# Sums of squares gathered in fewer steps, and the latent half of an output product kept out of the last banks

## What is computed

```python
def rms_norm(x, gain):
    y = xf * lax.rsqrt(jnp.mean(xf * xf, axis=-1, keepdims=True) + EPS)
    return (y * gain).astype(x.dtype)

# first block, each layer:
x = x + g1 * mixer(modulate(rms_norm(x, norm_gain[i, 0]), sh1, sc1))
x = x + g2 * swiglu(modulate(rms_norm(x, norm_gain[i, 1]), sh2, sc2), ffn_w_in[i], ffn_w_out[i])

# second block:
h = _rmsnorm(h_res, norm_w[l])
y_mla = _mla(...) * jax.nn.silu(g_mla)      # 1024 wide
y_na = _na(...) * jax.nn.silu(g_na)         # 1024 wide
h_res = h_res + jnp.concatenate([y_mla, y_na], axis=-1) @ w_out[l]
```

## Time and profile before

| | |
|---|---|
| time, median of 3 runs | 1233.76 us (1232.35 to 1234.3) |
| time of the profiled execution | 1234.3 us |
| its span, first to last instruction | 1232.6 us |
| mean granted TensorE clock | 0.991 of full speed |
| PE busy | 1177.3 us, 96% of the span |
| DVE busy | 706.9 us, 57% |
| ACT busy | 540.3 us, 44% |
| POOL busy | 92.9 us, 8% |
| DMA | 183.02 MB, mean 148 GB/s |

### The profile page before, as it was taken

How to read it: one execution, slowest core, us unless ns; L and a number is a source line. 1 busy time by engine, 2 the same in 40 slices (tenths; PEclk the granted TensorE clock), 3 DMA queues, 4 the chain that set the end, 5 groups by cost and what they waited for, 6 DMA issues and landing times.

```text
span 1232.6 us, 18590 instructions
## 1 busy us (share of the span) xinstructions
PE 1177.3 (96%) x7064; PEld 981.3 (80%) x7064; DVE 706.9 (57%) x1189; ACT 540.3 (44%) x1000; POOL 92.9 (8%) x137
## 2 busy tenths in 40 slices
PE   7999999999999999799998889999988999999998
PEld 4666687877878888577985789999987996799766
DVE  4534666766724333768569664455566475455673
ACT  3233422222223223544448654444446566466662
POOL 0002011122100000200000010000010000020410
PEclk9999999999999999899999999999999999999999
DMA  8889456578722223133330156565444443164220
GB/s 304 320 276 329 152 171 189 171 252 277 252 85 103 94 78 101 35 103 100 106 103 1 44 167 200 171 196 176 148 137 129 130 143 103 39 205 140 103 69 35
DMA packets 121670, 183.02 MB, mean 148 GB/s; under 512 B 4497, under 2 KB 92896, under 8 KB 121600
## 3 DMA queue, kind: packets, MB, share of 16 engines
q1 hardware_dynamic: 113888, 154.64, 38.2%
q0 software_dynamic: 7712, 27.43, 6.8%
HBM read 180.68 MB, written 1.05 MB: 147 GB/s over the span
## 4 chain that ended last, share of the span: by engine, by line
PE 83%; DVE 8%; ACT 4%; issue 3%; POOL 1%; DMA 0%; DVEq 0%; SPq 0%; ACTq 0%; POOLq 0%
PE ps L489 20%; PE ps L491 20%; PE ps L490 20%; PE ps L819 2%; PE ps L820 2%; PE ps L821 2%; PE ps L860 2%; PE ps L2201 1%; PE ps L2245 1%; ACT wh L467 1%; DVE wl L474 1%; DVE nm L1132 1%; PE ps L2533 1%; PE ps L2535 1%; DVE nrm L603 1%
## 5 line engine op out<-in xcount | busy, mean ns | idle before, releaser
L489 PE MATMUL ps<-hh,wh 128*128 128x256 f32 (+2 forms) x1272 | 425.7, 335 | 17.6 <-DVE hl L619 9.5
L474 DVE TENSOR_TENSOR wl<-raw,wh 128x1024 fp32r<-128x1024 f32 (+1 forms) x246 | 295.7, 1207 | 253.1 <-ACT wh L467 249.9
L490 PE MATMUL ps<-hl,wh 128*128 128x256 f32 (+2 forms) x1272 | 416.4, 327 | 0.0
L491 PE MATMUL ps<-hh,wl 128*128 128x256 f32 (+2 forms) x1272 | 415.4, 327 | 0.0
L467 ACT ACTIVATE wh<-raw 128x1024 fp32r<-128x1024 f32 (+1 forms) x246 | 252.6, 1032 | 272.9 <-PE ps L491 261.4
L489 PEld LDWEIGHTS ps<-hh,wh 128*128 128x128 f32 x1272 | 241.7, 190 | 59.8 <-issue 27.4
L490 PEld LDWEIGHTS ps<-hl,wh 128*128 128x128 f32 x1272 | 241.2, 190 | 22.6 <-issue 1.9
L491 PEld LDWEIGHTS ps<-hh,wl 128*128 128x128 f32 x1272 | 242.2, 190 | 21.1
L489 PE MATMUL ps<-ah,wh 128*128 128x256 f32 (+2 forms) x376 | 125.9, 335 | 1.1 <-DVE big L2018 0.8
L490 PE MATMUL ps<-al,wh 128*128 128x256 f32 (+2 forms) x376 | 124.2, 330 | 0.0
L491 PE MATMUL ps<-ah,wl 128*128 128x256 f32 (+2 forms) x376 | 124.2, 330 | 0.0
(11 more groups left out here) (241 smaller groups left out, 1442.4 us busy)
## 6 DMA issues: line engine op xcount, KB each, us to landing
raw<-in_ffn_w_in SPq DMA_DIRECT2D x44, 1024.0 KB, 5.2
raw<-in_ffn_w_out SPq DMA_DIRECT2D x22, 1024.0 KB, 4.9
raw<-in_w_in SPq DMA_DIRECT2D x22, 1024.0 KB, 5.3
big<-in_w_ada SPq DMA_DIRECT2D x16, 1024.0 KB, 9.5
big<-in_w_ada POOLq DMA_DIRECT2D x24, 512.0 KB, 4.4
ex<-in_w_ada POOLq DMA_DIRECT2D x24, 512.0 KB, 5.1
raw<-in_diff_w_in SPq DMA_DIRECT2D x12, 1024.0 KB, 5.1
raw<-in_w_out SPq DMA_DIRECT2D x8, 1024.0 KB, 4.9
```

The costliest lines, as they stand in the source:

```text
L474: ins = nc.vector.tensor_tensor(place(wl), v, place(wh).bitcast(F32), ALU.subtract)
L489: nc.tensor.matmul(o, w_hi, m_hi, start=first, stop=False, **kw)
L490: nc.tensor.matmul(o, w_hi, m_lo, start=False, stop=False, **kw)
L491: return nc.tensor.matmul(o, w_lo, m_hi, start=False, stop=last, **kw)
```

## The change

Two independent things.

1. For "ffn1" and "second" POOL adds up the squares of tiles 0 to 3 only (three additions). PE multiplies the sum in `norm_sum(3)`, called after output tile m = 5, the squares of tiles 4 and 5 in the calls after m = 6 and m = 7, and those of tiles 6 and 7 after the last tile. "ffn0" and "diff" stay as they are.
2. All eight latent halves go through bank 7, in two turns of four blocks (g = 0 to 7, each 12 matmuls): halves 0 to 3 for the four blocks in steps 5 to 12, six matmuls in every step; halves 4 to 7 for block 4 in steps 17 and 18, for block 5 in step 19, for blocks 6 and 7 after the loop. DVE adds every block into x: eight additions. Slots of halves 4 to 7 are counted as used in g = 7. The final banks begin with half 8.

```diff
-        GATHERED = ["ffn0", "diff", "ffn1", "second"]
-        N_ADDED = KD - 2
+        GATHERED = {"ffn0": KD - 2, "diff": KD - 2, "ffn1": KD - 4, "second": KD - 4}
...
-            if name in GATHERED and k >= 2:
+            if k >= 2 and name in GATHERED and k - 2 < GATHERED[name]:
                 act.wait_ge(s_added, added_before(name, max(k - 2, 1)))
             elif k >= 2:
                 act.wait_ge(s_sum, b + k - 1)
...
-            for k in range(1, N_ADDED):
+            for k in range(1, GATHERED[name]):
                 pool.wait_ge(s_sq, BASE[name] + k + 1)
...
-            if name in GATHERED and k < N_ADDED:
-                if k == N_ADDED - 1:
+            if name in GATHERED and k < GATHERED[name]:
+                if k == GATHERED[name] - 1:
                     pe.wait_ge(s_added, added_before(name, k))
...
-        PART_AT, parts = {}, [(g, k) for g in range(4) for k in range(4)]
-        for i in range(4, 15):
-            n = 1 + i % 2
-            PART_AT[i], parts = parts[:n], parts[n:]
-        assert not parts
+        PART_AT = {}
+        for x in range(8):
+            PART_AT.setdefault(5 + x, []).append(divmod(x, 2))
+        PART_AT.update({17: [(4, 0)], 18: [(4, 1)], 19: [(5, 0), (5, 1)]})
+        PARTS_IN = 6
         ROUND_AT = {2: [-2], 3: [-1], 13: [0], 14: [1], 15: [2], 16: [3]}
-        def latent_part(pe, g, k):
-
-            t, c = divmod(g, 2)
-            if g and k == 0:
+        def latent_part(pe, g, half):
+
+            turn, b = divmod(g, 4)
+            t, c = divmod(b, 2)
+            if g and not half:
                 pe.wait_ge(s_part, g)
...
+            for k in range(4 * turn + 2 * half, 4 * turn + 2 * half + 2):
+                q = OUT_Q + k
+                if b == 0:
+                    pe.wait_ge(split, q + 1)
...
+                nc.tensor.matmul(ps[:, 7, :], a_h, w_h, start=(k == 4 * turn), stop=False)
+                nc.tensor.matmul(ps[:, 7, :], a_h, w_l, start=False, stop=False)
+                ins = nc.tensor.matmul(ps[:, 7, :], a_l, w_h, start=False, stop=(k == 4 * turn + 3))
+                if b == 3:
+                    ins.then_inc(used, 1)
+            if half and b < 3:
                 ins.then_inc(s_fill, 1)
...
             na_dve(dve, link, mark)
-            split_next(dve, OUT_Q + 4, 8)
-            dve.wait_ge(s_part, 4)
+            latent_added(dve, 6)
+            split_next(dve, OUT_Q + 4)
+            latent_added(dve, 7)
+            split_next(dve, OUT_Q + 5, 7)
+            dve.wait_ge(s_part, 8)
...
-                if k >= 8:
-                    pe.wait_ge(s_os, NA_G0 + k - 8 + 1)
+                pe.wait_ge(s_os, NA_G0 + k - 8 + 1)
...
-                        nc.tensor.matmul(o, a_h, w_h, start=(k == 4), stop=False, skip_group_check=True)
+                        nc.tensor.matmul(o, a_h, w_h, start=(k == 8), stop=False, skip_group_check=True)
...
-            def na_tail(i):
-
-                if i > NA_STEPS:
-                    if i == NA_STEPS + 1:
-                        pe.wait_ge(s_mx, na_max_done(NA_STEPS - 1))
-                    out_half(i - NA_STEPS + 3)
-
-            na_pe(pe, na_tail)
-            for k in range(7, 16):
+            na_pe(pe, lambda i: None)
+            for g in range(PARTS_IN, 8):
+                for half in range(2):
+                    latent_part(pe, g, half)
+            for k in range(8, 16):
                 out_half(k)
```

More of the change, by code:

```diff
@@ L536, in build @@
                 "second": [(0, 0, L2)], "lat": [(2, 0, L), (3, L, HW)]}
-        GATHERED = ["ffn0", "diff", "ffn1", "second"]
-        N_ADDED = KD - 2
+        GATHERED = {"ffn0": KD - 2, "diff": KD - 2, "ffn1": KD - 4, "second": KD - 4}
         sq_acc = big[:, 13312:13824]
         def added_before(name, k):
-            return GATHERED.index(name) * (N_ADDED - 1) + max(k, 0)
+            base = 0
+            for other, added in GATHERED.items():
+                if other == name:
+                    return base + max(k, 0)
+                base += added - 1
         def norm_square(act, name, k):
@@ L650, in norm_sum @@
                     nc.tensor.matmul(ps[:, bank, 0:b - a], T["ones"], sq_acc[:, a:b], start=True, stop=False)\
-                        .then_inc(s_sum, N_ADDED)
+                        .then_inc(s_sum, GATHERED[name])
                 return
@@ L1279, in latent_part @@
                 pe.wait_ge(s_part, g)
[L1280 to L1292, removed]
+            for k in range(4 * turn + 2 * half, 4 * turn + 2 * half + 2):
+                q = OUT_Q + k
+                if b == 0:
+                    pe.wait_ge(split, q + 1)
+                n = slice(c * 512, (c + 1) * 512)
+                at = L2 + t * P
+                w_h, w_l = wh[:, q % SPLIT_SLOTS, n], wl[:, q % SPLIT_SLOTS, n]
+                a_h, a_l = hh[:, k, at:at + P], hl[:, k, at:at + P]
+                nc.tensor.matmul(ps[:, 7, :], a_h, w_h, start=(k == 4 * turn), stop=False)
[3 more added lines that the diff above has]
+                    ins.then_inc(used, 1)
@@ L1293, in latent_part @@
+            if half and b < 3:
                 ins.then_inc(s_fill, 1)
         def latent_added(dve, g):
-            if g == 3:
-                dve.wait_ge(used, OUT_Q + 4)
-            else:
-                dve.wait_ge(s_fill, g + 1)
-            tile = x_tok[:, g // 2, g % 2 * 512:(g % 2 + 1) * 512]
+            turn, b = divmod(g, 4)
+            if b == 3:
+                dve.wait_ge(used, OUT_Q + 4 * turn + 4)
+            else:
+                dve.wait_ge(s_fill, 3 * turn + b + 1)
@@ L1302, in latent_added @@
+            if turn:
+                dve.wait_ge(s_part, g - 3)
+            tile = x_tok[:, b // 2, b % 2 * 512:(b % 2 + 1) * 512]
             nc.vector.tensor_tensor(tile, ps[:, 7, :], tile, ALU.add).then_inc(s_part, 1)
@@ L1349, in na_pe @@
                     ins.then_inc(s_pv, 1)
-                for g, k in PART_AT.get(i, ()):
-                    latent_part(pe, g, k)
+                for g, half in PART_AT.get(i, ()):
+                    latent_part(pe, g, half)
                 tail(i)
@@ L1388, in na_dve @@
             for i in range(NA_STEPS + 6):
-                for g in range(4):
-                    if (g, 3) in PART_AT.get(i - 1, ()):
+                for g in range(PARTS_IN):
+                    if (g, 1) in PART_AT.get(i - 1, ()):
                         latent_added(dve, g)
@@ L2523, in out_half @@
                 pe.wait_ge(split, q + 1)
-                if k >= 8:
-                    pe.wait_ge(s_os, NA_G0 + k - 8 + 1)
+                pe.wait_ge(s_os, NA_G0 + k - 8 + 1)
                 for t in range(2):
-                    at = (L2 + t * P) if k < 8 else t * P
-                    a_h, a_l = hh[:, k % 8, at:at + P], hl[:, k % 8, at:at + P]
+                    at = t * P
+                    a_h, a_l = hh[:, k - 8, at:at + P], hl[:, k - 8, at:at + P]
                     for c in range(2):
```

## The result

The changed kernel takes 1241.88 us in the median of its runs (1240.16 to 1246.73) against 1234.57 us for the kernel before in the same comparison (1232.35 to 1235.86); the ratio is 1.007, 95% interval 1.005 to 1.0092, that is 6 to 11 us more. The profiled execution is the fastest one seen of it, 1238.1 us with a span of 1236.4. So a reading of its total alone would make the loss too small: the norm "diff", which the change doesn't touch, took 14.20 us from first square to logarithm in the profile before and 12.51 in this one, because the clock fell within it before and only 3.9 us behind it here. I compare stretch by stretch.

What follows compares the result with a forecast made beforehand. PE was busy 96% of the span, so the prediction counted where PE stands still. Its terms, 0.86 (ffn1) + 1.2 (second) + 3.5 (NA) + 1.0 (clock) = +6.6 us, gave 1240.3 us, range 1236.3 to 1243.

Steps and rivals of the forecast that it cites:

- the clock in NA: NA steps 14 to 16: 3.0 us of broken PE idle time brings the granted clock down, +1.0 us or nothing.
- the low end of "second": Norm "second" if PE's 1.9 us idle time leaves the clock at full level: logarithm at 917.25, -0.4 us.
- the hand-overs: Before blocks 5, 6 and 7: PE waits for DVE to empty bank 7, 3 x 0.93 = 2.8 us.
- the end of the kernel: After half 8 begins: the rest of the kernel is unchanged, no added time.
- ffn1, +0.86 us: Norm "ffn1": two multiplications of 0.43 us moved ahead of the last output tile delay the logarithm, +0.86 us.
- second: Norm "second": PE stands 1.9 us before the sum with two output tiles behind; low clock taken, +1.2 us.
- Steps 4 to 12: NA steps 4 to 12: 1.39 us stall goes, step 13 starts at 1182.8 against 1182.61, +0.2 us.
- Steps 13 to 18: NA steps 13 to 18: ACT and DVE hold the pace; PE waits 1.0 us before the product of step 18.
- Half 8's own wait: In block 7: half 8 cannot be rounded before half 4's slot is free, 0.5 us.
- The hand-overs are covered: Rival: blocks 5 to 7 begin without a wait, whole +0.8 us, 1234.6 us; chance 0.13, including otherwise not slower.
- The clock falls over the hand-overs: Rival: blocks 5 to 7 run wholly at the low clock level, +8.3 us, 1248.6 us; chance 0.05.
- The change does not shorten "second": Rival at "second": PE's stall moves to the third addition instead of going; included in the sum, no chance of its own.

Runs made afterwards that it cites:

- e3: The changed kernel with block 5 summed in bank 4 and block 6 in bank 5, so that no block waits for DVE: 1238.98 us, ratio 1.0042.
- e2: The kernel before with only the latent halves' part of the change, norms as before: 1238.52 us, ratio 1.0033.
- e4: The changed kernel with 21 unused matmuls filling PE's idle time in steps 15 and 16: 1241.43 us, ratio 1.0061.
- e8: The changed kernel profiled once more, nothing altered: one execution, 1244.53 us.
- e1: The kernel before with only the change to the norms "ffn1" and "second", output product as before: 1237.39 us, ratio 1.003.
- e6: The kernel before with its bank 7 parts dealt anew over steps 4 to 14, no block beginning in the step where one ends: 1231.99 us, ratio 0.9977.
- e9: The kernel before with only the norm "ffn1" changed to four squares summed on POOL: 1235.56 us, ratio 1.0011.
- e10: The kernel before with 7 unused matmuls behind output tile 6, ahead of the norm "ffn1": 1235.14 us, ratio 1.0014.
- e12: The kernel before with 28 unused matmuls behind output tile 6, ahead of the norm "ffn1": 1237.37 us, ratio 1.0033.
- e5: The kernel before with only the norm "second" changed to four squares summed on POOL: 1235.25 us, ratio 0.9996.
- e13: The changed kernel with 11 unused matmuls filling PE's idle time in step 4: 1240.05 us, ratio 1.0055.
- e14: The changed kernel with unused matmuls filling PE's idle time in step 4 and in steps 15 and 16: 1240.55 us, ratio 1.0053.

## Why the prediction was right in its direction and short in its sum

The direction was right and most steps were; the sum was +6.6 us, 1240.3 us, where the median came out at 1241.88, 7.3 us more than before, and the ratio, applied to 1234.57, at 1243.2, just above the range. The step that failed is the clock in NA: one drop behind steps 15 and 16, taken as certain at +1.0 us, and the wait of step 4 counted among the harmless ones. Beside it three sizes were off: the low end of "second" (-0.4, measured +1.04), the hand-overs (3 x 0.93, measured 3 x 1.06) and the end of the kernel (0, measured 0.12).

- **ffn1, +0.86 us**: 16.18 - 15.32 = 0.86. Right.
- **second**: the stall of 1.9 us before the sum came as said, and at the low level the cost was 0.9 to 1.2 us for the 1.2 predicted. Wrong was its other end, "-0.4 us at the full level". The time at that level was right, 917.25 - 908.43 = 8.82 us worked out and 8.80 measured (a slip in it, 915.1 + 0.5 set down as 915.8, did no harm), but it compared a changed norm at the full level with the old one at the low level, as if that level belonged to the old kernel. The old norm too runs at the full level in some executions, and then takes 7.76 us; the changed one takes 8.80, +1.04. At equal level this part gains in no profile.
- **Steps 4 to 12**: step 13 begins 29.09 us after step 3's turn (1182.57 - 1153.48); worked out were 1182.8 - 1153.82 = 29.0. Right, and so is that the stall of 1.39 us goes.
- **Steps 13 to 18**: from step 3's turn, the turn of piece 14 was worked out at 35.4 us and came at 35.32, the product of step 16 at 37.0 and came at 37.03, that of step 18 after the idle time at 40.9 to 41.0 and came at 40.98. That ACT and DVE hold these steps, and that the lead shrinks to 0.7 us there, was right.
- **Hand-overs, 3 x 0.93**: the mechanism right, the term too small: 1.06 each, because the first matmul behind a wait takes 0.1 us longer to its successor (1197.93 to 1198.26, 0.33 us, against 0.23). e3 shows that they cost 3.18 us and that nothing behind them takes their place. Half 8's own wait came about as said (0.38 us for 0.5). Half 8 begins 3.96 us later than before (3.5 predicted), and the end 0.12 us later still.
- **The clock in NA, +1.0 us, taken as certain**: the step that failed. It was taken because the idle time there, 3.0 us as worked out, was larger than at "diff"; the trace has 1.34 and 1.06 us with a turn between, neither as long as the 1.94 at "diff". Of the five profiles with the changed order of the blocks and the wait of step 4 unfilled (the first, e2, e3, e4, e8), two show low stretches, worth 3.5 us each time; in e4 steps 15 and 16 were filled. Only 0.6 of it lies behind steps 15 and 16. The rest, 2.9 us, is behind the 1.36 us wait of step 4, which every kernel has and which I had counted among the harmless ones, by the clock of 1.00 at the other wait of that length, 1.39 us. In kernels with the old order the same wait was also followed by a low stretch (e1, e6, e9, e10, e12), of 3 us in e1 and 1.5 us in the others, and in e5 one came behind step 16, 1.6 us. So the place that was taken as certain was one of several, and the rarer one.

At equal clock the change thus costs 0.86 + 1.04 + 3.96 + 0.12 = 5.98 us, where my terms without a drop gave 4.0. What is left to the measured 7.3 to 8.6 us, 1.3 to 2.6 us, goes together with a lower granted clock: 0.988 in the mean of the changed kernel's eight executions against 0.991 to 0.992 of before. Stretches at the low level that appear in some executions only, at "diff", at "ffn1", behind "second" and in NA, are worth 0.5 to 1.7 us each, the long ones of 6.8 us behind step 4 about 3, and the range had room for one of the short ones. Which of them the change makes more frequent is open, and with it the cause of this rest: filling steps 15 and 16 did not lower the time by more than the runs can tell, filling step 4 may have done so by 1 to 2 us (overlapping intervals), and no single part's clock explains the whole.

**The rivals.** "The hand-overs are covered" is refuted by e3. "The clock falls over the hand-overs" did not happen: in all six profiles of this order with one bank (the changed kernel, e2, e4, e8, e13, e14) the clock was back at its full level and stayed there from block 5 on. The Trainium skill's page "TensorE: Matmul & The Clock Gate", section "A second HAM failure mode: psum-queue depth-cycling", would let short idle times between groups bring the clock down; three hand-overs in a row, each with 0.78 us of idle time and PE busy for the rest, were not followed by the low level in any of these six, while the broken idle time in steps 15 and 16 was in e2 and e8 and not in the others. "The change does not shorten second" was right in both clock states.

## What to carry to other kernels

Before work is moved ahead of a wait, count what is queued behind it on the same engine: at "second" a wait that had stood behind the last product was moved in front of two output tiles, and the gain of two additions on POOL turned into a loss of 1.04 us, while with the wait left last the norm became 0.36 us shorter. A single accumulator bank that is emptied by another engine costs nothing only as long as the engine that fills it has other work during the hand-over, here 1.06 us; where that work runs out, take a second bank. And a stretch is to be compared with one at the same granted clock, since the level differs between executions of one kernel.

## What the runs showed of the hardware

The granted clock of one and the same kernel differs between executions: 0.984 to 0.992 for the changed kernel, and 1238.1 to 1246.73 us go with it, almost in order; 0.989 to 0.995 for the one before. Not all of the spread is the clock: up to the first square of "diff", where no two kernels differ and the level never fell, the eighteen profiles took 492.9 to 495.9 us. The same idle time (1.36 us before the product of step 4) came with a fall to the low level in seven of the fourteen profiles that have it unfilled, and PE busy 1.60 of 4 us (1187 to 1191) left it at full, where in e8 1.61 of 4 us (1192.85 to 1196.85) in the same steps were followed by the low level. The Trainium skill says on the page "TensorE: Matmul & The Clock Gate", section "Part 1: The HAM clock gate (the "warmup" mystery)", that the number of matmuls at the low level at a kernel's start differs between runs of the same kernel. The changed kernel's two profiles agree for places far behind the start: no low stretch in NA in the first, two in e8. Over all profiles such stretches cost 1.5 to 3.0 us from step 3 to half 8, and 0.6 us behind step 16 in the changed order, where PE had to wait anyway. One profile before and one after can differ by 1.7 us in a norm that no one has touched ("diff", 14.20 and 12.51).
